# A hybrid decoder block on eight cores: the first stage by chunks of all tokens, the final norm's squares summed in float32

## The reference

```python
h = rmsnorm(x, g_mix)
proj = h @ w_in                       # 3072 columns: u | v | z, 1024 each
u, v, z = gelu(proj[u]), gelu(proj[v]), proj[z]
out_a = u * (tril(w_s) @ rmsnorm_per_head(v, g_v) + b_s)    # in chunks of 128 positions
out_b = (trailing means of z over 2/4/8/16 positions - z) @ w_pool * pool_scale
x = x + concat(out_a, out_b) @ w_out
h = rmsnorm(x, g_ffn)
x = x + square(relu(h @ w_up)) @ w_down                     # width 8192
return rmsnorm(x, g_final)
```

## Time and profile before

| | us |
|---|---|
| median of 3 runs | 1242.95 (1240.61 to 1244.18) |
| the profiled execution | 1238.04 |
| its span, slowest core | 1236.2 |
| PE busy | 1193.5 (97%) |
| DVE busy | 354.9 (29%) |
| ACT busy | 221.0 (18%) |
| POOL busy | 78.8 (6%) |

### The profile page before, as it was taken

How to read it: one execution, slowest core, us unless ns; L and a number is a source line. 1 busy time by engine, 2 the same in 40 slices (tenths; PEclk the granted TensorE clock), 3 DMA queues, 4 the chain that set the end, 5 groups by cost and what they waited for, 6 DMA issues and landing times.

```text
span 1236.2 us, 14873 instructions; the slowest of 8 cores (1229.5 to 1236.2 us)
## 1 busy us (share of the span) xinstructions
PE 1193.5 (97%) x5880; PEld 571.5 (46%) x5984; DVE 354.9 (29%) x587; ACT 221.0 (18%) x446; POOL 78.8 (6%) x107
## 2 busy tenths in 40 slices
PE   4899999989999999999999999999999999999996
PEld 2354444434444444444444444444444444444585
DVE  3466646333322121111112121212121212121254
ACT  2401155133321100001111000111100011111233
POOL 0100022100000000000000000000000000010000
PEclk9999999999999999999999999999999999999998
DMA  9995640987533443344334443444334433446033
GB/s 271 232 183 76 83 83 2 145 168 173 127 69 68 83 88 68 68 77 93 70 69 73 91 76 68 70 86 83 69 68 85 85 69 69 81 81 111 26 125 124
DMA packets 36755, 118.59 MB, mean 96 GB/s; under 512 B 2768, under 2 KB 5200, under 8 KB 35664
## 3 DMA queue, kind: packets, MB, share of 16 engines
q0 software_dynamic: 22736, 87.04, 41.0%
q1 hardware_dynamic: 13376, 29.43, 7.5%
q10 hardware_dynamic: 576, 1.18, 0.3%
HBM read 196.28 MB, written 8.39 MB: 166 GB/s over the span
## 4 chain that ended last, share of the span: by engine, by line
PE 92%; DMA 5%; DVE 1%; issue 1%; SPq 1%; ACT 0%; DVEq 0%; ACTq 0%
PE ps L226 83%; PE ps L672 6%; DMA xstage<-xT 3%; DMA xf<-xT 2%; PE ps L412 1%; PE ps L896 1%; SPq L244 0%; PE ps L324 0%; PE ps L546 0%; DVE ostage L925 0%; PE ps L363 0%; SPq L248 0%; DVE xr_h L679 0%; PE ps L709 0%; DVE xr_h L883 0%
## 5 line engine op out<-in xcount | busy, mean ns | idle before, releaser
L226 PE MATMUL ps<-h2T,ringall 128*128 128x512 bf16 x2008 | 440.7, 379 | 2.1
L226 PEld LDWEIGHTS ps<-h2T,ringall 128*128 128x128 bf16 x2048 | 200.4, 98 | 241.6
L226 PE MATMUL ps<-pooled,ringall 128*128 128x512 bf16 (+1 forms) x989 | 212.1, 362 | 1.0
L226 PE MATMUL ps<-uT,ringall 128*128 128x512 bf16 (+1 forms) x992 | 212.1, 362 | 0.8
L804 DVE SCALAR_TENSOR_TENSOR rtmp<-ps,rstd_bc 128x512 f32<-128x512 f32 x128 | 82.4, 686 | 361.3 <-PE ps L226 350.0
L226 PEld LDWEIGHTS ps<-pooled,ringall 128*128 128x128 bf16 x1008 | 98.6, 98 | 101.9
L226 PEld LDWEIGHTS ps<-uT,ringall 128*128 128x128 bf16 x1008 | 98.5, 98 | 101.9
L809 ACT ACTIVATE uT<-rtmp 128x512 bf16<-128x512 f32 x64 | 39.1, 629 | 504.6 <-DVE rtmp L804 504.5
L226 PE MATMUL ps<-hT,ringall 128*128 128x512 bf16 x375 | 82.6, 379 | 0.6 <-issue 0.2
L809 ACT ACTIVATE pooled<-rtmp 128x512 bf16<-128x512 f32 x64 | 39.2, 629 | 181.8 <-DVE rtmp L804 181.8
L226 PEld LDWEIGHTS ps<-hT,ringall 128*128 128x128 bf16 x384 | 37.2, 98 | 44.4
(11 more groups left out here) (117 smaller groups left out, 624.6 us busy)
## 6 DMA issues: line engine op xcount, KB each, us to landing
ringall<-w_up POOLq DMA_DIRECT2D x32, 1024.0 KB, 8.0
ringall<-w_down POOLq DMA_DIRECT2D x29, 1024.0 KB, 7.9
ringall<-w_in POOLq DMA_DIRECT2D x10, 1024.0 KB, 12.6
xf<-xT SPq DMA_DIRECT2D x8, 1024.0 KB, 20.6
xstage<-xT SPq DMA_DIRECT2D x16, 512.0 KB, 10.0
ringall<-w_out POOLq DMA_DIRECT2D x7, 1024.0 KB, 17.2
wstg<-w_in SPq DMA_DIRECT2D x4, 1024.0 KB, 16.4
wres<-w_down POOLq DMA_DIRECT2D x3, 1024.0 KB, 22.1
```

What stands on the lines that cost most here:

```text
L226: ins = e.matmul(ps[:, banks[sel], c0:c1], lhsT, rhs, start=st, stop=sp_)
```

## The change

Stage one: x has one layout of all 1024 tokens by chunk k (in memory and in `xf`). The weights of the first three z tiles (`w_za`) and of the fourth (`w_zb`) have copies of their own in float32, laid out by chunk on the host. SP issues ten pairs of a piece of w_za and a piece of x, of one or two chunks (`PIECES`), then w_zb in four pieces, then the halo's x and invc. For each k PE does two statistics matmuls and six z matmuls (three tiles, two halves); after the last k rstd is made for both halves at once, and the fourth z tile follows by itself in banks 6 and 7, in four pieces. All eight z evictions of these tiles and the halo's two multiplies come after that on DVE. The fifth tile's weights are a load of one tile (`z4_ld`), that and the other half of slab 2 issued on POOL after the second piece of w_zb; slabs 3 and 4 and the constants after the fourth.

The xstage loads read the new layout: one run per partition instead of two.

Closing passes: the squares of tiles 0 to 13 are written in float32 and added up on DVE (`sqacc`), the sum is split into a bf16 hi and lo, and these two and the squares of tiles 14 and 15 are the only statistics matmuls of a pass. They are issued after the last tile's matmuls.

```diff
-    def load_x(half, q):
-        x_ld[half].append(P.dma("sp", lambda e: e.dma_start(
-            out=xf[:, half, KG * q:KG * q + KG, :], in_=xT_d[:, half, KG * q:KG * q + KG, :]), "x%d%d" % (half, q)))
-
-    for q in range(KC // KG):
-        wf_ld.append(P.dma("sp", lambda e, q=q: e.dma_start(
-            out=wstg[:, q, :, :].rearrange("p n (k c) -> p n k c", c=128), in_=w_in_d[:, 16:20, KG * q:KG * q + KG, :]), "wf%d" % q))
-        load_x(0, q)
...
+    PIECES = [0, 1, 2, 4, 6, 8, 10, 12, 14, 15, 16]
+    x_ld = [None] * KC
+    wa_ld = {}
+    wb_ld = {}
+    vecs_ld = cst1 = None
+    for k0, k1 in zip(PIECES, PIECES[1:]):
+        wa_ld[k0] = P.dma("sp", lambda e, k0=k0, k1=k1: e.dma_start(out=wsta[:, k0:k1, :], in_=w_za_d[:, k0:k1, :]), "wa%d" % k0)
+        ld = P.dma("sp", lambda e, k0=k0, k1=k1: e.dma_start(out=xf[:, k0:k1, :], in_=xT_d[:, k0:k1, :]), "x%d" % k0)
+        x_ld[k0:k1] = [ld] * (k1 - k0)
+        if vecs_ld is None:
+            vecs_ld = P.dma("sp", lambda e: e.dma_start(out=vecs[:, :], in_=vecs_d[:, :]), "cst0")
+    for k0 in range(0, KC, 4):
+        wb_ld[k0] = P.dma("sp", lambda e, k0=k0: e.dma_start(out=wstb[:, k0:k0 + 4, :], in_=w_zb_d[:, k0:k0 + 4, :]), "wb%d" % k0)
     for fn in (lambda e: e.dma_start(out=xh[:, :, :], in_=xh_d[:, :, :]),
                lambda e: e.dma_start(out=invc[:, :, :], in_=invc_d[:, :, :])):
         cst1 = P.dma("sp", fn, "cst1")
-    for q in range(KC // KG):
-        load_x(1, q)
-    wz_cast = [None] * (KC // KG)
 
...
-    nxt = [2]
+    nxt = [3]
...
             else:
-                deps.append(x_ld[1][1 if n == 2 else 3])
+                deps.append(wb_ld[KC - 4])
...
+    z4_ld = P.dma("pool", lambda e: e.dma_start(out=ringall[:, 4, :, :], in_=w_in_d[:, 16, :, :]), "z4", [wb_ld[4]])
+    slab_ld[2] = P.dma("pool", lambda e: e.dma_start(out=ringall[:, 5, :, :], in_=w_in_d[:, 17, :, :]), "slot2", [wb_ld[4]])
...
-    def stat_chunk(k, half, src_ap, src_deps, eng):
-        s = k % 4
+    sq_reader = [None] * 2
+
+    def stat_chunk(k, src_ap, src_deps, eng):
+        s = k % 2
         if eng == "act":
-            sq = P.add("act", lambda e: e.activation(out=sq_slot(s), in_=src_ap, func=AF.Square), list(src_deps) + [sq_reader[s]])
+            sq = P.add("act", lambda e: e.activation(out=sqr[:, s, :], in_=src_ap, func=AF.Square), list(src_deps) + [sq_reader[s]])
         else:
-            sq = P.add("dve", lambda e: e.tensor_tensor(out=sq_slot(s), in0=src_ap, in1=src_ap, op=ALU.mult), list(src_deps) + [sq_reader[s]])
+            sq = P.add("dve", lambda e: e.tensor_tensor(out=sqr[:, s, :], in0=src_ap, in1=src_ap, op=ALU.mult), list(src_deps) + [sq_reader[s]])
         d = [sq, ones_op]
...
-        pe = P.add("pe", lambda e: e.matmul(ps[:, 6 + half, :], ones[:, :], sq_slot(s), start=(k == 0), stop=(k == KC - 1)), d)
...
+            d += [bank_last[6], bank_last[7]]
+
+        def fn(e):
+            e.matmul(ps[:, 6, :], ones[:, :], sqr[:, s, 0:512], start=(k == 0), stop=(k == KC - 1))
+            return e.matmul(ps[:, 7, :], ones[:, :], sqr[:, s, 512:1024], start=(k == 0), stop=(k == KC - 1))
+        sq_reader[s] = P.add("pe", fn, d)
+        return sq_reader[s]
+
+    def rstd_chain(pe_op):
+        lns = []
...
+            c0, c1 = half * 512, (half + 1) * 512
+            bank_last[6 + half] = P.add("act", lambda e, half=half, c0=c0, c1=c1: e.activation(
+                out=rstd_bc[:, c0:c1], in_=ps[:, 6 + half, :], func=AF.Ln, bias=EPSB, scale=1.0 / D), [pe_op, eps_op])
+            lns.append(bank_last[6 + half])
+        return [P.add("act", lambda e, c0=c0: e.activation(out=rstd_bc[:, c0:c0 + 512], in_=rstd_bc[:, c0:c0 + 512], func=AF.Exp, scale=-0.5), [ln])
+                for c0, ln in zip((0, 512), lns)]
+
...
+    z_banks = [[take_bank(), take_bank()] for _ in range(ZA)] + [[6, 7]]
+
+    def h_chunk(k):
+        xk = xf[:, k, :]
+        hk = hT[:, k, :]
...
-    for half in range(2):
-        st = None
-        for k in range(KC):
-            q = k // KG
-            if half == 0 and k % KG == 0:
-                wz_cast[q] = P.add("dve", lambda e, q=q: e.tensor_copy(
...
-                d += [bank_last[b] for b in z_banks[half]]
-
-            def z_fn(e, half=half, k=k):
-                ins = None
-                for m in range(4):
-                    ins = e.matmul(ps[:, z_banks[half][m], :], ringall[:, m, k, :], hT[:, k, half * 512:(half + 1) * 512],
-                                   start=(k == 0), stop=(k == KC - 1))
-                return ins
-            z_job[half] = P.add("pe", z_fn, d)
...
+    def z_chunk(tiles, ks, deps):
+        def fn(e):
+            ins = None
+            for k in ks:
+                for m in tiles:
+                    for half in range(2):
+                        ins = e.matmul(ps[:, z_banks[m][half], :], ringall[:, m, k, :], hT[:, k, half * 512:(half + 1) * 512],
+                                       start=(k == 0), stop=(k == KC - 1))
+            return ins
+        if ks[0] == 0:
+            deps = deps + [bank_last[b] for m in tiles for b in z_banks[m]]
+        return P.add("pe", fn, deps)
+
+    st = za_job = zb_job = wa_cast = None
+    for k in range(KC):
+        if k in wa_ld:
+            k1 = PIECES[PIECES.index(k) + 1]
+            wa_cast = P.add("dve", lambda e, k=k, k1=k1: e.tensor_copy(
+                out=ringall[:, 0:ZA, k:k1, :].rearrange("p n k c -> p k n c"),
+                in_=wsta[:, k:k1, :].rearrange("p k (n c) -> p k n c", n=ZA)), [wa_ld[k]])
+        st = h_chunk(k)
+        za_job = z_chunk(range(ZA), [k], [wa_cast, h_ops[k]])
+    r1 = rstd_chain(st)
+    h_all = [h_ops[KC - 1], h_ops[KC - 2]]
+    wb_cast = None
+    for k in range(0, KC, 4):
+        wb_cast = P.add("dve", lambda e, k=k: e.tensor_copy(out=ringall[:, ZA, k:k + 4, :], in_=wstb[:, k:k + 4, :]), [wb_ld[k]])
+        zb_job = z_chunk([ZA], range(k, k + 4), [wb_cast] + h_all)
...
+    for m in range(ZA + 1):
+        for half in range(2):
+            z_evac_half(m, half, za_job if m < ZA else zb_job, z_banks[m][half])
+    sqh_op = P.add("dve", lambda e: e.tensor_tensor(out=sqh[:, :, :], in0=xh[:, :, :], in1=xh[:, :, :], op=ALU.mult), [cst1])
+    hh_all = P.add("dve", lambda e: e.tensor_tensor(out=hh[:, :, :], in0=xh[:, :, :],
+                                                    in1=vecs[:, G_MIX:G_MIX + KC].unsqueeze(2).broadcast_to([128, KC, HALO]), op=ALU.mult), [cst1, vecs_ld])
...
-                              [slab_ld[n]] + h_all)])
+                              [z4_ld if m == 4 else slab_ld[n]] + h_all)])
...
-        xs_ld[m] = P.dma("sp", lambda e: e.dma_start(out=xstage[m % 2][:, :].rearrange("p (h t) -> p h t", h=2), in_=xT_d[:, :, m, :]),
+        xs_ld[m] = P.dma("sp", lambda e: e.dma_start(out=xstage[m % 2][:, :], in_=xT_d[:, m, :]),
...
+    sqf_reader = [rt_readers[0], rt_readers[1]]
+    acc3 = [None]
+    add_wait, pend3 = [], []
+
+    def sq_slot3(n, T):
+        return sqr[:, n // 2, (n % 2) * 512:(n % 2) * 512 + T]
+
+    def stat3(sbank, T, slots, start, stop, deps):
+        def fn(e):
+            ins = None
+            for n in slots:
+                ins = e.matmul(ps[:, sbank, 0:T], ones[:, :], sq_slot3(n, T), start=start and n == slots[0], stop=stop)
+            return ins
+        pe = P.add("pe", fn, deps + [ones_op] + ([bank_last[sbank]] if start else []))
+        for n in slots:
+            hs_reader[n] = pe
+        return pe
+
+    def add_squares(i, m, sq):
+        t0, t1 = PASSES[i]
+        T = t1 - t0
+        acc3[0] = P.add("dve", lambda e: e.tensor_tensor(out=sqacc[:, t0:t1], in0=sqacc[:, t0:t1], in1=rtmp[:, m % 2, 0:T], op=ALU.add), [sq, acc3[0]])
+        sqf_reader[m % 2] = acc3[0]
+        if m == SQ_DIRECT - 1:
+            hi = P.add("dve", lambda e: e.tensor_copy(out=sq_slot3(0, T), in_=sqacc[:, t0:t1]), [acc3[0], hs_reader[0]])
+            lo = P.add("dve", lambda e: e.tensor_tensor(out=sq_slot3(1, T), in0=sqacc[:, t0:t1], in1=sq_slot3(0, T), op=ALU.subtract), [hi, hs_reader[1]])
+            pend3.append(lambda sbank=6 + i % 2: stat3(sbank, T, [0, 1], True, False, [hi, lo]))
...
-            if pending[0] is not None:
-                pending[0]()
+            if m == KC - 1:
+                while pend3:
+                    pend3.pop(0)()
             ev = P.add("dve", lambda e, m=m, b=banks[0], t0=t0, t1=t1, T=T: e.tensor_tensor(
                 out=XR(m)[:, t0:t1], in0=XR(m)[:, t0:t1], in1=ps[:, b, 0:T], op=ALU.add), [job, x2_ops[m], x2_e1[m], h2_ops[m]])
             bank_last[banks[0]] = ev
             x3_ops[i][m] = ev
-            hsl = hs_ctr[0] % 4
-            hs_ctr[0] += 1
-            sq_ap = sqr[:, hsl // 2, (hsl % 2) * 512:(hsl % 2) * 512 + T]
-            sq = P.add("act", lambda e, m=m, sq_ap=sq_ap, t0=t0, t1=t1: e.activation(out=sq_ap, in_=XR(m)[:, t0:t1], func=AF.Square), [ev, hs_reader[hsl]])
-
-            def mk(m=m, sq=sq, sq_ap=sq_ap, hsl=hsl, T=T, sbank=sbank):
-                d = [sq, ones_op]
```

(33 more changed lines are left out.)

80 lines of the change are left out of this document (24 added, 56 removed).

## The result

The changed kernel takes 1223.8 us, the median of runs from 1223.4 to 1224.0. The kernel before, beside it, took 1240.6 to 1244.2. The ratio is 0.9853, with a 95% interval of 0.9833 to 0.9873; of 1242.95 us that is 18.3 us (the two medians are 19.2 apart). The forecast was 1226.0, with a range of 1221 to 1235.

A forecast was written before the change was run, and what follows sets the result against it. The prediction took TensorE (PE), busy 97% of the span, as the bound. Terms of -6.8, -4.0 and -5.9 us sum to -16.7: 1221.3 us for the profiled execution, 1226 from the median, range 1221 to 1235.

The forecast's parts named there:

- stage one: Start of kernel: x by chunks lets PE keep up with loads, fifth z tile at 53.0 instead of 59.78, -6.8 us.
- xstage: Output projection: 4 KB runs make a load 4.3 to 5.4 us, PE stalls go, -4.0 us, bounds 0 and -5.1.
- closing passes: Closing passes: 14 statistics matmuls per pass leave PE's line, -5.9 us, bounds -5.2 and -6.1.
- T1: Stage one: moment the last x chunk lands, after 8 MiB of x and 3 of weights, taken as 42.8 us.
- The second term: Stage one: from the last chunk's landing to the fifth z tile's start, 10.1 to 10.3 us.
- PE is dry when the last chunk lands: Stage one: a chunk takes PE 1.73 us against 2.3 us of load, so no PE work is left at the last landing.
- the thin place: Stage one: fifth tile's weights land 9.8 us after the last chunk, wanted at 10.2; costed at 0, bounds -0 and +2.5.
- Rival E: Stage one: PE stays at half clock, kernel slower at 1251 us; a single slow stretch is caught up or costs 1.8; chance 0.05.
- Rival C: Stage one: small loads cost 0.5 us each over their bytes, +5 us, gain there only 1.8, total 1231 us; chance 0.12.
- the late weights: Stage one: fifth tile's weights 2.5 us late and PE restarting at half clock, also 1231 us; within a rival of chance 0.12.
- a landing of 14 us at most: Output projection, a sign to check: an xstage load lands within 14 us where 22.28 stood before.
- The same gain from the median: Whole kernel: the profiled execution's gain of 16.7 us taken from the shown runs' median of 1242.95, giving 1226 us.

The follow-up runs named there:

- 33 loads: Changed kernel with 16 single-chunk pieces in stage one instead of ten, 33 loads before the last landing instead of 21: 1224.1 us, ratio 0.9908 to the kernel before.
- 9 loads: Changed kernel with four pieces of four chunks in stage one, 9 loads before the last landing instead of 21: 1226.7 us, ratio 0.9929 to the kernel before.
- 1 KB run: Kernel before with each xstage load in 512 runs of 1 KB instead of 256 of 2 KB: 1243.3 us, ratio 1.0054 to the kernel before.

## Why the prediction was right, and where it was off

**The sum.** -16.7 was forecast for the profiled execution, and core 0, on which the terms were read, gave 15.3 (1236.2 to 1220.9). Term by term on core 0: stage one -6.8 forecast, -4.4 measured; xstage -4.0, -5.6; closing passes -5.9, -5.6. The first two misses nearly cancel, which is luck.

**Stage one, mis-sized in two terms.** T1 was worked out from core 0 alone as 42.8. It was 44.6 there and 45.5 on the slowest core, mean 44.2. The step that failed is the count of loads: eleven MiB were taken at 3.36 us each, with nothing for their pieces, while 0.13 us for each of ten more loads is by that estimate 1.3 us of the missing 1.8 on core 0, and nearly all of the 1.4 that the mean of the cores misses (in two other profiles of the same kernel the mean is 43.2, only 0.4 above the forecast, so this is good to 1 us). The rest is the spread between cores, up to 1.3 us beyond the mean, which nothing in the sum stood for: the slowest core's landing counts. The second term is the way from T1 to the fifth tile: 10.3 to 10.9 over the cores and 10.7 in the mean (up to 11.4 in another profile), against 10.1 to 10.3. The step said that PE is dry when the last chunk lands; it isn't. Chunk 14's six matmuls stand between, so the last chunk's statistics start at 47.20 instead of 46.6 on core 4. With 33 loads PE is dry on six of eight cores, and on these the way is the 10.3 of the working. Behind that all went as the working had it: the one wait is 0.27 us (0.3 forecast), the fourth tile 6.9, and the thin place, the fifth tile's weights, held: at most 9.0 us from issue on POOL, with no gap in front of 56.27. That DMA share is 0.07 in 46 to 50 on core 4 shows why: nothing else was left on the engines. The squares were nearly as costed (ACT 1.06 for "1.2, at most 1.4", DVE 1.23, h 0.75, cast 0.55).

**Rival E** happened in small, as its last sentence had it: one slow stretch, behind an idle of 3.33 us on core 0. PE has no idle from there to the 0.27 us of wait for rstd, and its fifth tile starts 10.8 us behind the landing, 0.5 more than the 10.3 of core 1, which had no such stretch; core 7, without one as well, took 10.6. The 1.8 us that the rival gave to a single stretch was seen as 1.7 with 9 loads. **Rival C** is refuted in size, and so is its other half, the late weights. The Trainium skill ("DMA: Bandwidth & Descriptors", Bandwidth) asks for loads of 1 MiB or more. The runs agree in direction only: the 9 large loads land 1.6 to 2.6 us before the changed kernel's 21 and their slowest fifth tile starts at 60.0, where the changed kernel has 56.3 at the latest, since here each load's size is also how much PE work is left when it lands. The fixed 2 us that the prediction took from the same page of the Trainium skill stands there in another section (Anatomy of one DMA) and for loads issued by GpSimd, not for those of SP that carry x.

**xstage, right in mechanism, under-sized.** In the working a 2 KB load took 8.6 us against 6.9 of PE per tile, and a 4 KB load 4.3 to 5.4. Measured: 369 ns and 225 ns per packet (71.2% of 352 us by 680, 31.1% by 486), so 8 x 0.594 = 4.75. The 1 KB run doubles the cause once more: 14.3 us, and a gap on every core. By the Trainium skill ("DMA: Bandwidth & Descriptors", Queues, rings and completion order) an engine goes round its queues packet by packet; the traces agree, with equal counts of both queues in each stretch of 4 us shown and one packet per 1, 2 or 4 KB run of this load. The check "a landing of 14 us at most" failed: the median is 10.9 us on the slowest core, but the longest is 17.0, more than two tiles of PE (13.8). It did no harm: PE can be three tiles ahead of the evictions, and it had no gap. The term's size was set at -4.0 because other cores would "keep a rest"; none did. On the slowest core it was worth 5.6 in the profiled pair, 5.9 by the table of core spans, and 4.1 taken out of the changed kernel.

**Closing passes, right, with both terms.** 14 matmuls per pass, 6.1 us by count; 5.6 came on both cores, and on the fastest core of the run with that part alone. The missing 0.5 us stands at the passes' ends, in the wait for hi and lo and the late eviction. From the last tile's matmuls to the pass's last statistics matmul it was 1.41 and is 1.85 us in the second pass (+0.44, forecast 0.2 to 0.4). In the last pass it was 1.40 and is 1.59 (core 0), in the first 1.95 and 1.83. Together +0.5. The checks held as well: a wait of 1.01 us in the first pass, tiles without a statistics matmul in their line, four of them per pass.

**From the profile to the median.** "The same gain from the median" was the other step that failed. The profiled execution of before (1238.04) lay below its timed runs (1240.6 to 1244.2), and in the later groups its runs went from 1232.6 to 1242.6 us. The spans of cores say what varies: the fastest core is at 1227 in each group, and the slowest carries 6 to 8 us of stalls that fall on another core in each run. Those stalls the change takes away, so its own time varies by 0.7 to 2.2 us within a group and the gain depends on which run of before stands beside it: 14.3 in the profiles, 18.3 beside the result, 15.0 and 13.1 later. That before was slower beside the result because of more or longer xstage stalls is the likely reading, but those runs left no trace; it stays open.

So 1226.0 came within 2.2 us by two errors of opposite sign, and that it came so near is luck: the profiled pair gained 14.3 where 16.7 was forecast, and before's median lay 4.9 us above its profile where the changed kernel's lies at it. The three mechanisms were right; two of their sizes and the step to the median were not.

## What to carry over

Where a load from a plain queue shares its engines with cast loads, its share is set by the length of its contiguous runs in memory: count the packets per engine of both queues and compare the turn with the compute that one load must cover, before looking for bandwidth. A stall that falls on a different core in each run hides from a profile of one core but not from the list of spans; take it as its own term, against the slowest core, and expect the gain to differ with the runs compared. Size the landing of a long series of loads from all cores and add a little for each load (0.13 us here), since the last piece and the slowest core set the time.

## What the runs showed of the hardware

- Where a plain queue and the cast queue both had packets for 4 us, the counts agreed within 6 packets on every core, at 1, 2 and 4 KB (150 to 148, 122 to 121, 129 to 131 on core 0). A cast packet (4 KB of bf16 written) took 365 to 391 ns of an engine in 228 to 250; packets of the float32 load took 81 ns at 1 KB, 145 at 2 KB and 225 at 4 KB. Twice the bytes cost about 1.6 to 1.8 times the time.
- 33 loads against 9 for the same 11 MiB moved the last landing from 41.6 to 44.8 us, 0.13 us for each load, at engines 99% busy in both. Loads and packet sizes changed together.
- With the same program on each core the last of 11 MiB lands 2.4 us apart (43.1 to 45.5); in two other profiles of it 2.6 and 1.3, with 33 loads 1.7.
- The granted clock fell to half behind some idle stretches of PE and not behind others of the same length. It fell behind 3.33 us in stage one (0.61 in 34 to 38), behind 5.37 us (0.50) and behind 2.07 us in the output projection, and behind 2.63 us with 9 loads (0.50). It stayed at 1.00 behind 2.69 us with 9 loads and behind 2.90 us in the kernel with xstage in 2 KB (16 matmuls in 3.61). So the length of the idle alone didn't decide it here. Where it fell, it cost 1.7 us in the earlier trace rows and from landing to fifth tile with 9 loads, and up to 2.7 behind the gaps of the 1 KB run.
